# Attention with keys before queries and values, and heads taken one by one

## The reference

```python
q, k, v = split(h @ w_in)               # q: 1024 columns, k: 256, v: 256
q = rope(rmsnorm(q per head) * q_g)     # rope on latent tokens only
k = rope(rmsnorm(k per head) * k_g)
keys, vals = concat(k_latent, k_context), concat(v_latent, v_context)
att_latent = softmax(q_latent @ keys.T * scale) @ vals       # both layers
att_context = softmax(q_context @ k_context.T * scale) @ v_context   # layer 0 only
```

## Time and profile before

| | |
|---|---|
| median of 3 runs | 2498.49 us (2498.09 to 2498.69) |
| the profiled execution: its own time, and its span | 2500.89 us, 2499.1 us |
| busy, TensorE / weight loads | 2335.4 us (93%) / 2062.4 us (83%) |
| busy, VectorE / ScalarE | 1508.4 us (60%) / 971.5 us (39%) |
| mean granted TensorE clock | 0.949 of full |
| the chain that ended last, by engine | TensorE 77%, VectorE 12%, ScalarE 4%, VectorE's queue 4% |
| costliest lines | 1839, 1840 and 1841 (products), 20% of the chain each |

### The profile page before, as it was taken

One profiled execution on the slowest core, in us unless ns is written; L12 is line 12 of the kernel. 1 busy time (PEld: TensorE's weight loads), 2 busy tenths in 40 slices (PEclk: granted clock), 3 DMA queues, 4 the chain that ended last, 5 costly groups with the idle time before them and its releaser, 6 DMA issues.

```text
span 2499.1 us, 34519 instructions
## 1 busy us (share of the span) xinstructions
PE 2335.4 (93%) x13618; PEld 2062.4 (83%) x13618; DVE 1508.4 (60%) x2766; ACT 971.5 (39%) x1533; POOL 34.1 (1%) x37
## 2 busy tenths in 40 slices
PE   7899999999999899999978999999889899989997
PEld 6788988788989888978866888888688789759996
DVE  6879986779985355554353434553454555456665
ACT  4555445654444433232323322222343434234342
POOL 0000000000000000000000000000001000000000
PEclk9899999999989899999979999999999999899998
DMA  5247855347853111123300333332131224305652
GB/s 185 91 146 255 273 174 160 100 143 261 271 187 115 49 35 34 36 76 93 93 9 12 98 95 99 95 100 94 54 99 35 59 60 148 97 9 177 177 177 85
DMA packets 177240, 284.65 MB, mean 114 GB/s; under 512 B 9460, under 2 KB 66932, under 8 KB 176824
## 3 DMA queue, kind: packets, MB, share of 16 engines
q1 hardware_dynamic: 174976, 276.60, 36.1%
q10 hardware_dynamic: 2104, 5.85, 0.7%
HBM read 281.37 MB, written 1.05 MB: 113 GB/s over the span
## 4 chain that ended last, share of the span: by engine, by line
PE 77%; DVE 12%; ACT 4%; DVEq 4%; issue 2%; DMA 1%; ACTq 0%; SPq 0%
PE bank L1839 20%; PE bank L1840 20%; PE bank L1841 20%; DVE WLO L914 3%; PE bank L2279 2%; PE bank L2217 2%; PE bank L2216 2%; PE bank L2044 1%; PE bank L2460 1%; PE bank L2480 1%; DVEq L1330 1%; DMA RAW<-in_e_w_in 1%; DVE ARENA L1327 1%; ACT WHI L464 1%; PE bank L2303 1%
## 5 line engine op out<-in xcount | busy, mean ns | idle before, releaser
L914 DVE TENSOR_TENSOR WLO<-RAW,WHI 128x1024 fp32r<-128x1024 f32 (+2 forms) x500 | 582.9, 1172 | 542.1 <-ACT WHI L464 529.1
L464 ACT ACTIVATE WHI<-RAW 128x1024 fp32r<-128x1024 f32 (+2 forms) x500 | 506.8, 1016 | 927.8 <-PE bank L1841 885.9
L1839 PE MATMUL bank<-ATH,WHI 128*128 128x256 f32 (+1 forms) x2032 | 661.7, 326 | 8.1 <-DVE ARENA L1467 2.1
L1840 PE MATMUL bank<-ATL,WHI 128*128 128x256 f32 (+1 forms) x2032 | 655.2, 322 | 0.0
L1841 PE MATMUL bank<-ATH,WLO 128*128 128x256 f32 (+1 forms) x2032 | 655.1, 322 | 0.0
L1839 PEld LDWEIGHTS bank<-ATH,WHI 128*128 128x128 f32 x2032 | 390.3, 192 | 41.4 <-DVE ARENA L1572 2.2
L1840 PEld LDWEIGHTS bank<-ATL,WHI 128*128 128x128 f32 x2032 | 390.2, 192 | 28.2
L1841 PEld LDWEIGHTS bank<-ATH,WLO 128*128 128x128 f32 x2032 | 389.9, 192 | 28.6
L1839 PE MATMUL bank<-WHI,ATH 128*128 128x512 f32 (+2 forms) x900 | 320.9, 357 | 9.9 <-DVE WLO L914 6.7
L1840 PE MATMUL bank<-WLO,ATH 128*128 128x512 f32 (+2 forms) x900 | 316.4, 352 | 0.0
L1841 PE MATMUL bank<-WHI,ATL 128*128 128x512 f32 (+2 forms) x900 | 315.9, 351 | 0.0
(11 more groups left out here) (279 smaller groups left out, 2768.2 us busy)
## 6 DMA issues: line engine op xcount, KB each, us to landing
RAW<-in_w_in SPq DMA_DIRECT2D x192, 512.0 KB, 3.7
RAW<-in_w_ff SPq DMA_DIRECT2D x128, 512.0 KB, 4.8
ARENA<-in_w_ada SPq DMA_DIRECT2D x64, 384.0 KB, 5.0
RAW<-in_o_w_in SPq DMA_DIRECT2D x24, 512.0 KB, 4.0
RAW<-in_e_w_in SPq DMA_DIRECT2D x16, 512.0 KB, 4.7
RAW<-in_w_ple_gate SPq DMA_DIRECT2D x16, 512.0 KB, 4.0
RAW<-in_w_br_gla SPq DMA_DIRECT2D x16, 512.0 KB, 3.6
RAW<-in_w_br_attn SPq DMA_DIRECT2D x16, 512.0 KB, 3.6
```

The costliest lines, as they stand in the source:

```text
L464: nc.scalar.activation(WHI[:, slot, 0:n], RAW[:, slot, 0:n], ACT.Copy).then_inc(hi_split, 1)
L914: V.tensor_tensor(WLO[:, slot, 0:n], RAW[:, slot, 0:n], WHI[:, slot, 0:n], ALU.subtract).then_inc(lo_split, 1)
L1839: mm(o, ah, bh, start=start, stop=False, skip_group_check=free)
L1840: mm(o, ah, bl, start=False, stop=False, skip_group_check=free)
```

## The change

1. **Order of the products.** K comes first, then the two Q products, then V. The same weights are loaded, in the new order.
2. **The norms in two parts.** The keys' squares are summed and the keys rotated on TensorE between the two Q products; VectorE makes the roots, the diagonals and the key rotation there, and TensorE spreads the scales after the third slot of the second Q product (`after={2: key_scales}`), now into banks 6 and 7. The queries' squares are summed between the second Q product and the V product, and VectorE's roots for them, and the first head's rotation, are placed inside the V product's stretch. `SQK` and `DIAG` move to other places of the memory. TensorE waits for the V copies before the first scores.
3. **Heads one by one.** In step n TensorE makes the scores of head n, the transposes of head n-1, the rotation of head n+1 and the product with the values of head n-1. VectorE: gain n+1, division n-1, maxima n, store n-2, rotation n+1. ScalarE: copies of the transposes of n-1, exponentials of n. Heads still alternate between banks 0 to 2 and 3 to 5; the product with the values goes to bank 6 and the rotation to bank 7.

The core of the diff, cut:

```diff
@@ second_plan
-            (f"q{n}", 2, [std(w, C_Q, BLK)]), (f"k{n}", 1, [std(w, C_K, width=AKV * AD)]),
+            (f"k{n}", 1, [std(w, C_K, width=AKV * AD)]), (f"q{n}", 1, [std(w, C_Q + half * BLK) for half in range(2)]),
@@ ScalarE
-                segment(f"q{layer}", [4], square_heads(SQQ, 4, tq))
                 segment(f"k{layer}", [AKV], square_heads(SQK, AKV, TOK))
+                segment(f"q{layer}", [4, 4], square_heads(SQQ, 4, tq))
                 segment(f"v{layer}", [4])
...
-                for _ in range(AH // 2):
-                    attend()
+                for n in range(AH + 1):
+                    if n:
+                        turned_out((n - 1) % 2)
+                    if n < AH:
+                        exps_of(n % 2)
@@ VectorE
+                groups(0, lambda n, c: head_in(KG[:, c, :], c, TOK), AKV)
+                drain()
+                V.tensor_scalar(KG, KG, col("k_norm_g_2", layer), None, ALU.mult).then_inc(a_gain, 1)
+                groups(0, query_in)
+                key_scales()
+                base = T.now(gemm_step)
+                lo(SLOTS - 1)
+                keys_done()
+                for c in range(4):
+                    dve.wait_ge(gemm_step, base + 4 * (SLOTS - 1) + c + 1)
+                    query_in(1, c)
+                lo(1)
...
+                lo(1)
+                query_scales()
+                lo(SLOTS - 2)
+                for c in range(TT):
+                    dve.wait_ge(gemm_step, base + TT * (SLOTS - 1) + c + 1)
+                    freed(V.tensor_copy(VA[:, c, :], bank[c][:, 0:AKV * AD]), c)
+                lo(1)
...
+                for n in range(AH + 2):
+                    if n + 1 < AH:
+                        gain(n + 1)
+                    if 1 <= n <= AH:
+                        divide((n - 1) % 2)
+                    if n < AH:
+                        maxima(n)
+                    if n >= 2:
+                        stored(n - 2)
+                    if n + 1 < AH:
+                        rotate((n + 1) % 2)
@@ TensorE
-                loop_blocks(2, lambda: cols_product(4, AT, tq))
-                cols_product(AKV, AT, TOK, wcols=AKV * AD)
-                rows_product(AKV * AD)
...
+                cols_product(AKV, AT, TOK, wcols=AKV * AD)
+                cols_product(4, AT, tq)
+                key_sums()
+                cols_product(4, AT, tq, after={2: key_scales})
+                query_sums()
+                rows_product(AKV * AD)
+                rotated(bank[7][:, 0:S], QS[:, 0, 0:S])
+                for b in bank_free[0:TT]:
+                    pe.wait_ge(b, T.now(b) + 1)
...
+                def values(hd, kv):
+
+                    r, v = hd % 2, [VA[:, s, kv * AD:(kv + 1) * AD] for s in range(TT)]
+                    pe.wait_ge(a_pt, T.next(a_pt))
+                    if hd:
+                        pe.wait_ge(a_stored, T.next(a_stored))
...
+                for n in range(AH + 1):
+                    if n < AH:
+                        scores(n % 2, n * AKV // AH)
+                    if n:
+                        turn_probs((n - 1) % 2)
+                    if n + 1 < AH:
+                        rotated(bank[7][:, 0:S], QS[:, (n + 1) % 2, 0:S])
+                    if n:
+                        values(n - 1, (n - 1) * AKV // AH)
+                pe.wait_ge(a_stored, T.next(a_stored))
```

More of the change, by code:

```diff
@@ L1703, in _ @@
[L1703 to L1712, removed]
-                last.then_inc(a_diag, 1)
-                drain()
-                V.tensor_tensor(KG[:, :, 0:S], KG[:, :, 0:S], ROTW, ALU.add)
-                drain()
-                dve.wait_ge(a_bc, T.next(a_bc))
-                for kv in range(AKV):
-                    V.tensor_tensor(K2[:, kv, :], KG[:, kv, :], bank[5 - kv][:, :], ALU.mult)
@@ new lines, in keys_done, with query_scales @@
+                def keys_done():
+                    dve.wait_ge(a_bc, T.next(a_bc))
+                    for kv in range(AKV):
+                        V.tensor_tensor(K2[:, kv, :], KG[:, kv, :], bank[6 + kv][:, :], ALU.mult)
+                def query_scales():
+                    dve.wait_ge(a_sums, T.next(a_sums))
+                    V.tensor_scalar(RSV[:, 0:AH * nq], bank[4][:, 0:AH * nq], 1.0 / AD, EPS, ALU.mult, ALU.add)
+                    gain(0)
+                    drain()
+                    rsqrt(RSQ[:, 0:AH * nq], RSV[:, 0:AH * nq], RSW[:, 0:AH * nq])
+                    V.tensor_scalar(RSQ[:, 0:AH * nq], RSQ[:, 0:AH * nq], ATTN_SCALE, None, ALU.mult)
+                    rotate(0)
@@ new lines, in maxima @@
+                def maxima(hd):
+                    r = hd % 2
+                    dve.wait_ge(a_score, T.next(a_score))
+                    for t in range(nq):
+                        sc = bank[3 * r + t][:, :] if t < NT else bank[3 * r + 2][:, (t - NT) * S:(t - NT + 1) * S]
+                        V.tensor_reduce(NM[:, r, t:t + 1], sc, AX, ALU.max, negate=True)
+                    V.tensor_copy(SCL[:, r, 0:nq], RSQ[:, bass.ds(hd * nq, nq)])
+                    drain()
+                    V.tensor_tensor(NM[:, r, 0:nq], NM[:, r, 0:nq], SCL[:, r, 0:nq], ALU.mult).then_inc(a_max, 1)
@@ new lines, in divide, with stored @@
+                def divide(r):
+                    dve.wait_ge(a_exp, T.next(a_exp))
+                    V.reciprocal(RD[:, r, 0:nq], DN[:, r, 0:nq])
+                    drain()
+                    for t in range(nq):
+                        pr = PL[:, r, t, :] if t < NT else PC[:, r, t - NT, :]
+                        last = V.tensor_scalar(pr, pr, RD[:, r, t:t + 1], None, ALU.mult)
+                    last.then_inc(a_norm, 1)
+                def stored(hd):
+                    dve.wait_ge(a_out, T.next(a_out))
+                    V.tensor_copy(QG[:, bass.ds(hd * TOK, tq)], bank[6][:, 0:tq]).then_inc(a_stored, 1)
@@ new lines, in turn_probs @@
+                def turn_probs(r):
+                    pe.wait_ge(a_norm, T.next(a_norm))
+                    for t in range(NT):
+                        for s in range(TT):
+                            last = turn(bank[3 * r + t][:, s * P:(s + 1) * P], PL[:, r, t, s * P:(s + 1) * P], ident)
+                    for t in range(nq - NT):
+                        for s in range(NT):
+                            last = turn(bank[3 * r + 2][:, t * S + s * P:t * S + (s + 1) * P], PC[:, r, t, s * P:(s + 1) * P], ident)
+                    last.then_inc(a_turned, 1)
```

198 lines of the change are left out of this document (81 added, 117 removed).

## The result

| | before | after |
|---|---|---|
| median of 4 runs each, in turn on one chip | 2498.59 us (2498.09 to 2499.95) | 2485.9 us (2481.62 to 2488.07) |
| the profiled execution: its own time, and its span | 2500.89 us, 2499.1 us | 2487.0 us, 2485.2 us |
| busy, TensorE / VectorE / ScalarE | 2335.4 / 1508.4 / 971.5 us | 2323.4 / 1511.4 / 970.4 us |
| mean granted TensorE clock | 0.949 | 0.954 |
| the chain that ended last | TensorE 77%, VectorE 12% | TensorE 77%, VectorE 11% |

The ratio is 0.9945 with an interval of 0.9933 to 0.9957: 12.7 us faster, where 20.6 had been forecast. The time lies inside the range of 2465 to 2491 us, but outside the 2472 to 2483 that had the chance of 0.60.

A forecast was written before the change was run, and what follows sets the result against it. TensorE, busy 93% of the span, was taken to bound the kernel. Gains of 3.9 + 2.8 (norm stretches) and 8.6 + 5.3 (loops) made 20.6 us, so 2478 us; forecast 2472 to 2483 (chance 0.60), range 2465 to 2491.

The forecast's parts named there:

- Layer 0's step: Steady loop step per head, set by TensorE's scores, transposes, waited-for copies and values: 8.6 us in layer 0.
- Rival 2: Clock falls after the scores in each step of layer 0, 8.5 us lost; 2486 us; chance 0.17 with mixtures.
- rival 3: Clock stays low through much of both loops, adding 65 us, 2543 us if it lasted; chance 0.04.
- the bubble in each step: Idle gap in every loop round, which by the skill's clock rule speaks against the change; full clock was forecast nonetheless.
- Rival 4: In-order queues block the loop's overlap, steps cost 10.7 and 7.4 us, only 6.7 us gained; 2492 us; chance 0.07.
- Rival 1: Clock holds everywhere, in V, first scores and layer 0's query sums; gain 31.3 us, 2467 us; chance 0.12.
- The norm stretches: From last product before attention to first scores: 26.7 to 22.8 us in layer 0, 19.2 to 16.4 in layer 1.
- query sums: One-column records before the V product: 64 in layer 0, 9.9 us; 32 in layer 1, 3.6 us.
- V at the low clock: V product starts at 1.2 GHz behind the query sums; half speed for 4 us loses 2.0, bounds 0 and 2.5.
- the key chain: VectorE's key roots and diagonals, 6.8 us, covered by 8.6 us of Q product; a stall would cost up to 5 us a layer.
- The mis-sized term: Low clock at the first scores of each loop, after 5 idle us: 2.0 us added, between 0 and 4.
- The full-clock sums: Loop times before the low-clock addition: first two steps, six steady steps and the end; 75.3 us in layer 0.

The follow-up runs named there:

- the filled run: Changed kernel plus 22 extra matmuls, results unused, while TensorE waits for the V copies before the first scores; 2477.0 us, 0.9913 of the kernel before.
- the loop that is at the full clock from end to end: Kernel with shorter ring and query sums in two runs, plus 12 or 8 unused matmuls in step 0's wait for head 1's rotation; 2455.02 us, 0.9829.
- the loop alone: New head-by-head loop after the old product order and old norms, against the kernel before; 2485.37 us, ratio 0.995.
- the early rotation: Changed kernel with head 0's rotation matmul inside the V product, its VectorE operations after the second weight split, two splits behind the V copies; 2468.34 us, 0.9879.
- the late rotation: Changed kernel with VectorE's wait and three operations for head 0's rotation moved behind two weight splits and four V copies; 2468.76 us, 0.988 of the kernel before.
- the two parts: Each part alone against the kernel before: new product order and norms with the old loop, 2492.52 us, 0.9975; new loop with old norms, 2485.37 us, 0.995.
- The split run: Kernel with the shorter ring, query sums of heads 0 to 3 moved inside the second Q product; 2457.36 us, 0.9841 of the kernel before.

## Why the prediction came out as it did

**The mechanism held.** Layer 0's step was forecast at 8.6 and took 8.46 us, layer 1's at 5.95 and took 5.81 (2189.66 to 2195.47); TensorE's one repeated wait is on ScalarE's copies, 1.31 and 0.81 us. Rival 2 and rival 3 needed a clock that falls in the steps; it was 1.00 in all steady ones, so neither came. That the time, 2485.9, is the one given for rival 2 (2486) is chance. The Trainium skill, page "TensorE: Matmul & The Clock Gate", section "Loop structure matters more than you think", sets matmuls back to back against a long wait ahead of every matmul; the prediction read the bubble in each step as speaking against this loop. It did not here: the row over five steps, with a wait of 1.31 us in each, has 1.00. What a longer one would do in each step no run shows. Rival 4 needed a division or a maximum that TensorE waits for in each step; none is there. Rival 1 failed on the idle stretch and on the one-column sums.

**The norm stretches.** The terms of layer 0 as measured: key sums 1.7 and rotation 0.5 (forecast 1.8 and 0.9), key scales 1.7 (1.9), wait for Square 0.69 (0.6), query sums 10.6 (9.9), V at the low clock 1.4 (2.0: the V product took 12.95 us, from 1252.95 to 1265.90, where 96 matmuls at 0.12 make 11.5), and 5.74 from the last V matmul to the scores (5.7). These make 22.3 against the forecast 22.8, with some 0.4 us between the rows, and the stretch gained 3.95 us against 3.9. That it is so near is in part luck: sums that took 0.7 more were offset by a V product that lost 0.6 less and a rotation that held TensorE 0.4 less. In layer 1 the sums took 3.6 us, V lost 1.55 and the last term was 5.75: gain 3.5 against 2.8. Nothing stalls inside the second Q product, so the key chain kept its cover.

**The mis-sized term** is the clock behind the new idle stretch, 2.0 us in each loop with a bound of 4. By the filled run it cost 3.2 us in layer 0 and 4.3 in layer 1: 1.8 in the first step (6.61 us against 4.81), 0.9 in the second (8.49 against 7.56) and 1.6 in the last values. That the 1.6 belong to the idle stretch is not shown, since the same place was slow and then fast in two executions of the kernel before. Against the loop that is at the full clock from end to end 2.4 us more are left (52.74 against 50.36), but that kernel also stores earlier, so not all of it is clock. The full-clock sums behind the term were good: 75.3 and 51.7 forecast, 74.66 and 52.74 measured, the latter still with slow second scores. Steps 0 and 1 of layer 0, forecast at 15.4, took 15.5 in the filled run and 18.7 in after, which is the 3.2. The row used for the bound, the first scores of layer 1 in the kernel before, stood behind 2.71 us of idling, and I read it as the whole of the cost. But the first two steps are not steady ones: TensorE waits again in step 0 for head 1's rotation, which VectorE makes behind head 0's maxima, so the clock stays low or falls a second time, and the second scores are slow as well. I had also priced the 5.7 us of waiting at its own length and had seen that TensorE would be idle, yet gave the clock the price of a gap half as long. The length alone would not have told it either: with the loop alone, behind 2.71 us in both layers, the loop of layer 0 cost as much as in after.

**Outside attention** I had put nothing, and the span lost 3.5 us there. Of it 2.7 us lie ahead of attention. Over all twelve traces attention starts between 1174.74 and 1182.90 us, with two traces of the same kernel 5.2 us apart, so this is the spread of single executions. The rest, 1.0 less the 0.1 won at the end, lies between the attentions, where no instruction differs, and the granted clock has a part in it. A stretch of 50 us that starts 450 us after the loop of layer 0, in after and then in the filled kernel:

```profile
1799.51:1849.51 50.00, 41.70 (x292) 40.15 (x292) 31.17 (x76) 19.91 (x33) 0.00 (x0) 0.90 0.28 81
```
```profile
1797.03:1847.03 50.00, 41.78 (x312) 40.10 (x313) 32.08 (x75) 20.01 (x34) 0.00 (x0) 0.97 0.33 98
```

Twenty more matmuls in the same time; but in the next 50 us the clocks are the other way round (0.91 and 0.84). Added up over windows of 25 us, TensorE spends some 65 us at 1.2 GHz between the attentions in after and 61 in the filled kernel. By an estimate from these, 4 us at half the speed are worth 2 us, and the two kernels differ by 3.5; the kernel before has 61 us at the low clock too, and takes 755.9. So the clock explains at most a part, and the rest stays open. The work between the attentions takes 756.9 us in both traces of after and in that with the early rotation, 753.3 to 753.9 with the loop alone, the late rotation and the filled idle time, 755.2 to 756.0 in the others. So 3.5 us of the 9.8 that the filled version gains on after come from here. It is also why the two parts don't add up (6.2 us and 12.5 us alone, some 12 together, by the ratios): in attention they gain 6.6 and 12.7, 19.3 against 17.4 together, between the attentions 0.1 and 2.0, where together they lose 1.0, and the last 1.5 us or so are within the intervals. What in the earlier work changes these later stretches wasn't tried and stays open.

So the sum was 20.6; the loop of layer 1 gave 3.3 less, that of layer 0 0.6 less, the norms 0.8 more, and 3.5 went outside: with rounding 13.9 in the traces, and 12.7 in the medians. Against the second trace of the kernel before, the loop of layer 1 gave 5.0 less than forecast instead of 3.3.

## What to carry to other kernels

Price a wait of TensorE ahead of dense work at its length and at what the next matmuls lose to the low clock, and ask whether the steps behind it are steady or have waits of their own; if the wait can't be removed, spare products in a free bank can keep the clock (here they cost nothing that the norm stretches show, 0.01 us). When an in-order engine stands in such a wait for one operation, look at what is queued behind it: here two splits that nobody needed were in the way of the copies, and moving three small operations behind them gained 14.4 us in attention, beside the 17.4 of the whole edit. Once a pipelined step is steady, its one repeated wait tells what a shorter ring is worth: handing over a part early took away 1.0 of 1.3 us. And take a second trace of the kernel before: one of its four stretches moved by 1.7 us between two, nearly all of the 2.0 read off as a gain there.

## What the runs showed of the hardware

One-column matmuls keep TensorE busy, yet the granted clock falls in them. In layer 0 of after the query sums start at 1242.37; TensorE and its weight loads are busy all along:

```profile
1242.00:1245.00 3.00, 2.63 (x24) 2.63 (x24) 1.29 (x2) 0.83 (x2) 0.00 (x0) 1.00 0.13 14
1245.00:1253.00 8.00, 8.00 (x43) 8.00 (x43) 0.00 (x0) 0.00 (x0) 0.00 (x0) 0.55 0.18 60
1253.00:1256.00 3.00, 3.00 (x15) 3.00 (x16) 0.00 (x0) 0.00 (x0) 0.00 (x0) 0.50 0.00 0
1256.00:1258.00 2.00, 2.00 (x19) 2.00 (x18) 0.00 (x0) 0.54 (x1) 0.00 (x0) 0.99 0.03 8
```

That is a clock of 1.2 GHz for some 10 us, 3 of them in the dense V product behind. The split run shows that 32 records with dense work on both sides bring it down as well. Idling is not alike either: steady waits of 1.31 us in each 8.46 us, with transposes between, left the clock at 1.00 in every step, while it fell in 3.00 us ahead of the second scores of layer 0 in one kernel (early rotation, 3.44 us for the scores) and not in 3.09 us at the same place in another (late rotation, 1.98 us). So the length of the wait alone doesn't explain it, and these runs don't say what does.
